# The hybrid block's modulation vector, summed into columns instead of a row

## What is computed

```python
c_act = jax.nn.silu(c)                       # (1, 1024)
mod = c_act @ w_ada + b_ada                  # (1, 3072)
shift, scale, gate = jnp.split(mod, 3, axis=-1)
h = rmsnorm(h_res, norm_w) * (1.0 + scale) + shift
y = hybrid_mixer(h, ...)
h_res = h_res + gate * y
```

## Time and profile before

| | us |
|---|---|
| median of three runs | 1892.86 (1890.5 to 1892.97) |
| the profiled execution's own time | 1890.38 |
| its span | 1888.6 |
| PE busy in the span | 1861.2 (99%), 9993 instructions |
| DVE, ACT, POOL busy | 978.3, 616.1, 557.0 |
| granted clock of PE | 0.999 of full speed |

### The profile page before, as it was taken

How to read it: one execution, slowest core, us unless ns; L and a number is a source line. 1 busy time by engine, 2 the same in 40 slices (tenths; PEclk the granted TensorE clock), 3 DMA queues, 4 the chain that set the end, 5 groups by cost and what they waited for, 6 DMA issues and landing times.

```text
span 1888.6 us, 26587 instructions
## 1 busy us (share of the span) xinstructions
PE 1861.2 (99%) x9993; PEld 1536.3 (81%) x9993; DVE 978.3 (52%) x2103; ACT 616.1 (33%) x1303; POOL 557.0 (29%) x927
## 2 busy tenths in 40 slices
PE   7999999999999999999999999999999999999998
PEld 7888888888888788888888787888887777788886
DVE  5556465774666433114777322223213777776665
ACT  6321111233444432101222202221114666555552
POOL 2112232232642221110101000222314777544442
PEclk9999999999999999999999999999999999999999
DMA  6313242356897845312221124665563677867663
GB/s 184 107 67 117 72 127 78 109 173 236 311 265 248 251 149 165 106 49 85 70 81 67 51 62 118 205 214 173 167 220 103 214 215 270 271 218 240 229 229 112
DMA packets 236365, 303.54 MB, mean 161 GB/s; under 512 B 41415, under 2 KB 161127, under 8 KB 236205
## 3 DMA queue, kind: packets, MB, share of 16 engines
q1 hardware_dynamic: 205724, 215.84, 37.0%
q0 software_dynamic: 23600, 77.61, 11.4%
q10 hardware_dynamic: 6912, 8.39, 1.2%
HBM read 194.71 MB, written 107.54 MB: 160 GB/s over the span
## 4 chain that ended last, share of the span: by engine, by line
PE 94%; DMA 2%; DVE 1%; issue 1%; ACT 1%; POOL 0%; SPq 0%; POOLq 0%; ACTq 0%; DVEq 0%
PE banks L145 26%; PE banks L147 26%; PE banks L146 26%; PE banks L2079 3%; PE banks L2042 3%; PE banks L2061 2%; PE banks L2677 2%; PE banks L2679 1%; PE banks L2370 1%; DMA iraw<-in_w_in 1%; PE banks L2647 1%; PE banks L2062 1%; PE banks L234 1%; PE banks L1083 1%; DMA hd<-nkl 0%
## 5 line engine op out<-in xcount | busy, mean ns | idle before, releaser
L145 PE MATMUL banks<-hT,wu 128*128 128x512 f32 (+1 forms) x528 | 205.5, 389 | 4.0 <-DVE hT L220 4.0
L147 PE MATMUL banks<-hT,wu 128*128 128x512 f32 (+1 forms) x528 | 203.1, 385 | 0.0
L146 PE MATMUL banks<-hT,wu 128*128 128x512 f32 (+1 forms) x528 | 203.0, 384 | 0.0
L145 PE MATMUL banks<-iT,wub 128*128 128x512 f32 x384 | 151.2, 394 | 0.0
L145 PE MATMUL banks<-iT,wua 128*128 128x512 f32 x384 | 150.8, 393 | 0.0
L145 PE MATMUL banks<-wub,iT 128*128 128x512 f32 x384 | 150.6, 392 | 0.0
L147 PE MATMUL banks<-iT,wub 128*128 128x512 f32 x384 | 149.7, 390 | 0.0
L147 PE MATMUL banks<-iT,wua 128*128 128x512 f32 x384 | 149.5, 389 | 0.0
L146 PE MATMUL banks<-wub,iT 128*128 128x512 f32 x384 | 149.5, 389 | 0.0
L146 PE MATMUL banks<-iT,wua 128*128 128x512 f32 x384 | 149.5, 389 | 0.0
L147 PE MATMUL banks<-wub,iT 128*128 128x512 f32 x384 | 149.5, 389 | 0.0
(11 more groups left out here) (289 smaller groups left out, 4100.8 us busy)
## 6 DMA issues: line engine op xcount, KB each, us to landing
iraw<-in_w_in SPq DMA_DIRECT2D x36, 512.0 KB, 4.3
wa<-in_w_ada SPq DMA_DIRECT2D x48, 256.0 KB
yT<-sg POOLq DMA_DIRECT2D x32, 256.0 KB, 3.1
oraw<-yT SPq DMA_DIRECT2D x32, 256.0 KB, 4.4
xr<-in_x SPq DMA_DIRECT2D x16, 512.0 KB, 3.9
h<-h POOLq DMA_DIRECT2D x16, 512.0 KB, 3.8
hT<-tr POOLq DMA_DIRECT2D x16, 512.0 KB, 4.7
tws<-wg SPq DMA_DIRECT2D x16, 512.0 KB, 5.0
```

What stands on the lines that cost most here:

```text
L145: e.matmul(ps, lh, rh, start=first, stop=False)
L146: e.matmul(ps, lh, rl, start=False, stop=False)
L147: return e.matmul(ps, ll, rh, start=False, stop=last)
```

## The change

The sum over the partitions is turned round. What was one matmul with ones as weights and 512 moving columns becomes four matmuls for each block, in which a 128x128 quarter of `acc` is the weights and the single column of ones is the moving operand. Each gives a column of 128 sums, so the block's 512 sums stand as four columns over 128 partitions. The bias is loaded once, as 24 columns, into a tile of its own (`bcol`), at unit 17; DVE adds a 128x4 piece of it to the sums and writes a tile of its own (`mcol`); POOL stores those four columns to the same places in `k.mod`. The `wa` buffers carry nothing but slices of `w_ada` now, so their loads wait for `acc_step` alone.

```diff
--- before.py
+++ after.py
@@ -258,6 +258,7 @@
         self.gb, self.sc = k.at("gb", 197.03125, [P, KT]), k.at("sc", 197.0625, [P, KT])
         self.c, self.ones = k.at("c", 197.09375, [P, KT]), k.at("ones", 197.125, [P, 2])
         self.nw = k.at("nw", 197.15625, [P, KT])
+        self.bcol, self.mcol = k.at("bcol", 197.1875, [P, 24]), k.at("mcol", 197.28125, [P, 24])
         self.acc, self.wa = k.at("acc", 198, [P, W]), [k.at(f"wa{i}", 200 + 2 * i, [P, W]) for i in range(2)]
         self.zb, self.z = k.at("zb", 204, [32, 17, 40]), k.at("z", 207, [32, 64])
         self.pa = banks[7]
@@ -270,7 +271,7 @@
         self.halo_out, self.pooled = k.sem("halo_out"), k.sem("pooled")
         self.wt_turned, self.wt_hi, self.wt_lo, self.wp_full, self.wp_out = (k.sem(n) for n in ("wt_turned", "wt_hi", "wt_lo", "wp_full", "wp_out"))
         self.y_step, self.y_out, self.sg_st = k.sem("y_step"), k.sem("y_out"), k.dsems("sg_st", 3, "pool")
-        self.c_in, self.wa_in, self.silu_c, self.acc_step = k.dsem("c_in"), k.dsems("wa_in", 2), k.sem("silu_c"), k.sem("acc_step")
+        self.bcol_in, self.c_in, self.wa_in, self.silu_c, self.acc_step = k.dsem("bcol_in"), k.dsem("c_in"), k.dsems("wa_in", 2), k.sem("silu_c"), k.sem("acc_step")
         self.summed, self.mod_out, self.mod_st = k.sem("summed"), k.sem("mod_out"), k.dsem("mod_st", "pool")
         self.z_out, self.rpb_st, self.zb_in = k.sem("z_out"), k.dsem("rpb_st", "pool"), k.dsem("zb_in")
         self.zb_step, self.zb_st = k.sem("zb_step"), k.dsem("zb_st", "pool")
@@ -296,7 +297,7 @@
         self.ada_steps, self.sum_at, self.bias_at = {n: [] for n in range(64)}, {}, {}
         for j in range(6):
             for x in range(8):
-                self.ada_steps[14 + 8 * j + x // 2].append(9 * j + x)
+                self.ada_steps[14 + 8 * j + x // 2].append(8 * j + x)
             self.sum_at[20 + 8 * j], self.bias_at[21 + 8 * j] = j, j
         self.tables = {b: [] for b in range(16)}
         for i in range(16):
@@ -335,19 +336,12 @@
 
         def ada(i):
 
-            j, x = i // 9, i % 9
-            sl = slice(j * W, (j + 1) * W)
+            j, x = i // 8, i % 8
             if i == 0:
                 w.wait_ge(*norm.turned.ge(2 * NT))
             if i >= 2:
-                if (i - 2) % 9 < 8:
-                    w.wait_ge(*self.acc_step.ge((i - 2) // 9 * 8 + (i - 2) % 9 + 1))
-                else:
-                    w.wait_ge(*self.mod_st.ge((i - 2) // 9 + 1))
-            if x < 8:
-                e.dma_start(self.wa[i % 2][:], io["w_ada_2"][0][x * P:(x + 1) * P, sl]).then_inc(*self.wa_in[i % 2].inc())
-            else:
-                e.dma_start(self.wa[i % 2][0:1, :], io["b_ada_2"][:, sl]).then_inc(*self.wa_in[i % 2].inc())
+                w.wait_ge(*self.acc_step.ge(i - 1))
+            e.dma_start(self.wa[i % 2][:], io["w_ada_2"][0][x * P:(x + 1) * P, j * W:(j + 1) * W]).then_inc(*self.wa_in[i % 2].inc())
 
         def table(i):
             a, h = i // NA_H, i % NA_H
@@ -384,8 +378,8 @@
                 gate_weights(g + 1)
             for i in self.ada_steps[n]:
                 ada(i)
-            if n in self.bias_at:
-                ada(9 * self.bias_at[n] + 8)
+            if n == 17:
+                e.dma_start(self.bcol[:], io["b_ada_2"][0].rearrange("(q p) -> p q", p=P), allow_slow_non_contiguous=True).then_inc(*self.bcol_in.inc())
             if n % 4 == 3:
                 for i in self.tables[n // 4]:
                     table(i)
@@ -526,13 +520,17 @@
                 if j:
                     w.wait_ge(*self.summed.ge(j))
                 e.tensor_scalar(acc[:], wa[:], self.c[:, 0:1], None, ALU.mult).then_inc(*self.acc_step.inc())
-            elif x < 8:
+            else:
                 w.wait_ge(*self.acc_step.last())
                 e.scalar_tensor_tensor(out=acc[:], in0=wa[:], scalar=self.c[:, x:x + 1], in1=acc[:],
                                        op0=ALU.mult, op1=ALU.add).then_inc(*self.acc_step.inc())
-            else:
-                w.wait_ge(*self.summed.ge(j + 1))
-                e.tensor_tensor(wa[0:1, :], self.pa[0:1, :], wa[0:1, :], ALU.add).then_inc(*self.mod_out.inc())
+
+        def biased(j):
+
+            qs = slice(4 * j, 4 * j + 4)
+            w.wait_ge(*self.bcol_in.ge(1))
+            w.wait_ge(*self.summed.ge(j + 1))
+            e.tensor_tensor(self.mcol[:, qs], self.pa[:, 0:4], self.bcol[:, qs], ALU.add).then_inc(*self.mod_out.inc())
 
         def pool(g, tb, a):
             b = 4 * g + tb
@@ -624,7 +622,7 @@
             for i in self.ada_steps[n]:
                 ada(i)
             if n in self.bias_at:
-                ada(9 * self.bias_at[n] + 8)
+                biased(self.bias_at[n])
             if n % 4 >= 2:
                 self.gate(e, w, b, n % 4 - 2)
             out.ahead_dve(e, w, n)
@@ -711,7 +709,8 @@
             if n in self.bias_at:
                 j = self.bias_at[n]
                 w.wait_ge(*self.mod_out.ge(j + 1))
-                e.dma_start(k.mod[:, j * W:(j + 1) * W], self.wa[(9 * j + 8) % 2][0:1, :]).then_inc(*self.mod_st.inc())
+                e.dma_start(k.mod[0, j * W:(j + 1) * W].rearrange("(q p) -> p q", p=P), self.mcol[:, 4 * j:4 * j + 4],
+                            allow_slow_non_contiguous=True).then_inc(*self.mod_st.inc())
             if n % 4 == 3:
                 for i in self.tables[b]:
                     table(i)
@@ -766,7 +765,9 @@
                     w.wait_ge(*self.mod_out.ge(j))
                 else:
                     w.wait_ge(*norm.lo.ge(2 * NT))
-                e.matmul(self.pa[0:1, :], self.ones[:, 0:1], self.acc[:], start=True, stop=True).then_inc(*self.summed.inc())
+                for q in range(4):
+                    t = e.matmul(self.pa[:, q:q + 1], self.acc[:, q * P:(q + 1) * P], self.ones[:, 0:1], start=True, stop=True)
+                t.then_inc(*self.summed.inc())
 
     def turn_weights(self, e, w, g, s):
```

## The result

The changed kernel takes 1900.48 us (median of 5 runs, 1900.16 to 1903.52), the kernel before on the same chip 1890.5 (5 runs, 1889.01 to 1892.97). The ratio is 1.0052, its 95% interval 1.0042 to 1.0063. The forecast was 1890.1 with a range up to 1895.5, so both the time and the sign are wrong. The profiled execution of the changed kernel took 1900.16 us with a span of 1898.3, 9.7 more than the span before.

What follows compares the result with a forecast made beforehand. PE was taken as the bound, busy 1861.2 of 1888.6 us. Six sums at -0.26 us each gave -1.6, DVE, SP and POOL nothing: 1891.7 - 1.6 = 1890.1 us, range 1887.0 to 1895.5.

Steps and rivals of the forecast that it cites:

- PE, what is removed and added: In PE's six column sums, 1.147 us each goes and 0.88 comes, no gap: -0.26 each, -1.6 us in all.
- rival 4: In the new sums, passes of one column take 0.055 us, not 0.11; six gain 4.2 us: 1887.5; chance 0.08.
- rival 2: In each sum the four matmuls don't overlap and pay 0.507 us each, 2.03 a sum: 1897.0; chance 0.08.
- DVE, and SP's column load: DVE's bias addition gets shorter; SP's one load of 3072 pieces lands in 5 to 10 us; both cost nothing.
- POOL: POOL's store of 512 four-byte pieces may take 10.4 us to land, at most 0.92 to issue; hidden, cost nothing.
- What SP loses is more interesting: On SP's queue, slice loads lose 87.0 us of waits for the stored row and go earlier; PE gains nothing.
- the first paragraph of the prediction: A microsecond off PE's stream shortens the end; one off another engine is worth nothing until PE waits for it.
- Where PE could meet a wait: Two tight places, block 5's sum (slack 0.5 us) and the next stage's last `ys` tiles (2 us); no wait expected.
- a wait of PE for `acc` between 150 and 430 us: A sign that the prediction is wrong: PE waiting for the accumulated slices in the stretch that makes the modulation.
- Rival 3: DVE's last slices or first `ys` tiles come late, DMA queues crowded by small pieces: 1892 to 1894; chance 0.08.

Runs made afterwards that it cites:

- e1: The changed kernel with each store packed as 128 runs of 16 bytes, mod stored in permuted order: 1888.99 us, ratio 0.9990.
- e10: The changed kernel with each store's 512 pieces of 4 bytes laid 24 bytes apart, mod in permuted order: 1889.69 us, ratio 0.9989.
- e11: The changed kernel with each store's 512 pieces 64 bytes apart in a separate scratch, readers taking the bias instead: 1888.97 us, ratio 0.9985.
- e16: The changed kernel with its 24 columns kept on chip, transposed once on PE behind product 63, stored as 24 runs of 512 bytes: 1888.82 us, ratio 0.9989.
- e2: The kernel before plus, behind each row store, an extra store of 512 neighbouring 4-byte pieces that nothing reads: 1932.47 us, ratio 1.0220.
- e4: The kernel before plus, behind each row store, an extra store of one column, 128 neighbouring 4-byte pieces: 1925.95 us, ratio 1.0186.
- e9: The kernel before plus, in the extra store's place, a load of 512 neighbouring 4-byte pieces from the bias: 1891.04 us, ratio 1.0000.

## Why the prediction was wrong, step by step

**PE, what is removed and added: right.** The changed kernel at its first sum:

```profile
159.78 0.95 PE L769 MATMUL banks<-ones,acc 128*128 128x1 f32 x8
```

The matmul before it stands at 159.55 and L146 behind it at 160.91, so a sum takes 1.36 - 0.453 = 0.907 us where 0.88 was forecast and 1.147 stood before; no gap, and passes of one column are not faster than 0.11 (rival 4 falls, and rival 2 with it). The four versions without close pieces and without a new wait (e1, e10, e11, e16) shorten the stretch of the six sums by 1.5 to 1.6 us, where 1.6 was forecast; as whole executions they lie 1.9 to 2.8 us under the kernel before (ratios of 0.9985 to 0.9990).

**DVE, and SP's column load: right.** The addition takes 0.15 us instead of 0.67. `bcol` landed in 4.5 us, half a microsecond under the 5 to 10 of the forecast, and nothing was late for it.

**POOL: the step that failed.** It said that the piecewise store "may take as long as `bc`'s 10.4, and nothing but the end of the stage waits for it". Its landing was about as given, 9.0 us, and nothing does wait for it. The error is the conclusion, cost nothing. A store was priced by who waits for its end, and not by what else needs the DMA engines meanwhile. e2 and e4 charge it 34 to 41 us with nothing else changed; e1, e10 and e11 take away only its closeness and the 10 us with it. The rows on which I leaned, `cw` and `bc`, are loads, and e9 shows that a load of the same pieces costs nothing. The trace of before has no store of neighbouring 4-byte pieces, and that should have widened the range.

**"What SP loses is more interesting": wrong in its effect.** SP no longer waits for the store of `mod`, as said, and DVE's total wait for `wa` went down a little (23.6 us before, 18.5 after). But the longest went from 4.5 to 7.3, at a place where SP's queue is in order and everything for the next stage stands behind it. And where the slices are free and no pieces lie close (e1, e10, e11), PE's stretch is shorter by the sums' 1.6 us and no more: what SP gained was worth nothing to PE, as the first paragraph of the prediction would have it.

**Where PE could meet a wait: the place right, the reason wrong.** The last sum, with its 0.5 us of slack, is one of the two; I expected DVE's run to come earlier there, and it came 9.7 us later. The waits for `wu` in blocks 2 and 4 were on no list. The prediction had named a wait of PE for `acc` between 150 and 430 us as a sign that it is wrong, and this one came. Rival 3, a new wait because queues are crowded by small pieces, is nearest to what happened, though it is not small pieces as such but close ones being written. It had a chance of 0.08 and a price of 1892 to 1894; it had neither the waits for `wu` nor the clock, which took 3.4 us.

## What to carry to other kernels

Ask of a store not only who waits for it but what is issued behind it, on any queue, while it is under way; and price a store from rows of stores, not of loads. Columns that lie across partitions should not be written as neighbouring 4-byte numbers: pack what one partition holds, lay the pieces apart, or turn the columns on PE first, as e16 does for one transpose. And where PE is the bound, a wait can cost more than it lasts: here each of the two longest, 2.11 and 3.07 us, brought about 1.7 us more by the lower clock, and those up to 1.22 us brought none.

## What had not been expected of the hardware

- 128 neighbouring pieces of 4 bytes, 512 bytes in all, take 8.8 us to land and cost this kernel 34 us in six stores; the same pieces 512 bytes apart land in 1.7 us and cost nothing.
- With the pieces 24 bytes apart the store landed in 4.1 us, and there was no loss.
- Loads of 256 KB that left at most 0.4 us behind such a store landed in 2.6 to 2.8 us in nine cases of twelve; those that left 0.9 to 5.8 us behind it, in 6.7 to 11.7. The DMA engines were not busy meanwhile: 22 GB/s and a busy share of 0.25 from 375 to 380 us.
- DVE's operations with one float32 operand read 32 bytes apart took over 1.7 times as long (1285 to 2217 and 1225 to 2149 ns for 128x1024).
